# A two-block hybrid layer on one core: modulation tiles in four column groups, x queued behind two weight tiles, one statistics product

## The chip, the cores and the metric

One core of a Trainium2 chip. The metric is the device time of one execution in microseconds (us), the median of several runs. A profile comes from one execution, taken by the hardware profiler, and its span runs from the first to the last instruction. Engine names: PE is TensorE (matmuls), PEld its weight loads, DVE is VectorE, ACT is ScalarE, POOL is GpSimd, SP is SyncE, which here only issues DMAs. A letter q behind an engine means its queue.

## What is computed

Two transformer-like blocks over a sequence of 512 with width 1024, batch 1, all in f32. The change lies in the first steps of the first block, which are:

```python
cond = jax.nn.silu(c)
mod = cond @ w_ada[l] + b_ada[l]                      # 1024 -> 3072
shift, scale, gate = jnp.split(mod, 3, axis=-1)
h = rms_norm(x, norm_g[l]) * (1.0 + scale[:, None, :]) + shift[:, None, :]
proj = h @ w_in[l]
```

`proj` is split into the inputs of a state-space mixer (S5), of an attention with selected keys (an indexer scores the keys, the top 128 are kept), and of gates. The S5 mixer needs exp(lambda * dt) of complex parameters, and so a sine and a cosine of 1024 arguments. The rest of the first block and the second block (retention, gated linear attention, sliding-window attention, merging and a gated feed-forward) aren't touched by the change. `rms_norm` divides each position by the root of the mean of its squares over the width, plus an epsilon.

## The kernel before, in words

**Layout.** Activations are kept turned: the width lies on the 128 partitions in eight slabs (KT = 8) of 512 positions. All weights arrive as one stream of tiles of 1024 KB (128 partitions x 8 slabs x 256 columns), in the order of the list STAGES (line 64). The stream goes through three slots, `w_raw` (RAW_SLOTS = 3): SP issues the load of tile i when tile i - 3 has been used (L445 to L459). The first eight tiles are the shift and scale columns of `w_ada`, multiplied as they come ("raw"); of the others ACT makes a rounded high half (`split_high`, L1129) and DVE the rest (`split_low`, L1681), and a product is three matmuls: high by high, high by low, low by high. The first split tile is that of the key index (k_idx).

**Order of the work.** Each engine has its own program, written out by hand, and engines wait for each other by counting semaphores. Nothing reorders the work of an engine.

- **SP** (L435 to L464) issues ten small loads, then x (`xr`, 2048 KB, L443), then the stream (L445, L457).
- **POOL** (L468 to L511) sets constants, stores the small table of the relative bias (`bias_dram`), spreads it to 128 rows in DRAM (`bias_rows`, 2560 KB, L477), and then waits for the projected input of the state space (`u_act`).
- **PE** (L655 to L694): two products for the bias table into banks 4 and 5; then eight modulation tiles. `ada_rows` (L610) multiplies one tile: eight matmuls with one column of `silu_c` as weights and 256 moving columns; the result is one row on partition 0. Behind tile 0 stand the statistics products of slabs 0 to 3 of x (`stats_of`, L633: a 128x128 matrix of ones times the squares, which gives the sum over the width on all partitions), behind tile 1 those of slabs 4 to 7. Behind each odd tile from 3 on, `modulation` (L624) waits for ACT's copy of a finished pair of tiles (`mod_row`) and turns its 512 numbers from a row to columns, four matmuls with `turned` (L618). Then comes the product of k_idx (L672 to L687), each of whose eight steps waits for its slab of h (`act_low`), and the whole for the low half of its tile (`w_low`). The program's one matmul in f32 shows as two instructions in the trace.
- **ACT** (L1163 to L1192): the silu of c (L1164), two copies of the bias table, then eight squares of x into two buffers (`sqb`, L1143; the third waits until PE has used the first, and so on), then the two sines (L1174, L1175), for which DVE waits, then four row copies (`mrow`, L1185) with the root of the statistics behind the first, and the high halves of h (`input_high`, L1180) two by two, with the cast of the first split tile between the sixth and the seventh.
- **DVE** (L1721 to L1882): the S5 parameters up to the argument of the sines (L1721 to L1736), a wait for the sines (L1737), the rest of the setup up to `bb_im` (L1738 to L1765), the powers of lambda (L1767 to L1778), the reciprocal `rstd` (L1701), and a loop over four pairs of slabs (L1848): bias and gain (`modv`, `gs`), the values (`tval`, L1858) and, one slab behind, the low halves of h (`input_low`, L1844). The low half of the first split tile is made in its third round (L1862).

`PRESUM` (L329) lists the norms whose squares are added on DVE so that PE makes one product of the sum; norm0 isn't in it.

Of the kernel before, what the change touches and what calls it, by code (L numbers as in the profile page):

```python
# [19 lines left out]
P = 128  # L20
SEQ = 512
D = 1024
KT = D // P
TT = SEQ // P
WC = 256
# [131 lines left out]
def hybrid_blocks(nc, wstream, xT, vecs, consts, head_rows, onehot, rel_bias, ssm_vec, ssm_b, ssm_c, d_skip,  # L157
# [13 lines left out]
    with ctx:  # L171
# [48 lines left out]
        def placed(*tensors):  # L220
# [7 lines left out]
        (h_hi, h_lo, win_re, win_im, bb_re, bb_im, b_re, b_im, c_re, c_im, sv, pw_re, pw_im, tmp, btab, mrow, grow,  # L228
# [13 lines left out]
            (F0 + 74 * K, "mrow", [1, 2048], f32), (F0 + 48 * K, "grow", [1, 512], f32),  # L242
# [56 lines left out]
        c_ready, ada_done, mod_ready = sem("c_ready"), sem("ada_done"), sem("mod_ready")  # L299
# [29 lines left out]
        PRESUM = ("norm1", "post1", "norm2", "post2")  # L329
# [106 lines left out]
        def _(sp):  # L436
# [6 lines left out]
            sp.dma_start(xr[:, :, :], xT).then_inc(in_x, 16)  # L443

            for i, (kind, n, (_, _, kt, _)) in enumerate(STREAM):  # L445
                if kind == "split" and n == G["out1"][1].s:

                    sp.wait_ge(lg_ready, 32)
                    sp.dma_start(xr[:, :, :], xT).then_inc(x_reload, 16)
                if i >= RAW_SLOTS:  # L450
                    was, k, _ = STREAM[i - RAW_SLOTS]

                    if was == "split":
                        sp.wait_ge(*tile_used(k))
                    else:
                        sp.wait_ge(raw_used, k + 1)
                sp.dma_start(w_raw[:, i % RAW_SLOTS, 0:kt, :],  # L457
                             wstream[i][:, 0:kt * WC].rearrange("p (t c) -> p t c", c=WC)
                             ).then_inc(raw_loaded[i % RAW_SLOTS], 16)  # L459
# [8 lines left out]
        def _(pool):  # L468
            pool.memset(ones[:, :], 1.0).then_inc(consts_set, 1)
# [6 lines left out]
            pool.wait_ge(bias_stored, 16)  # L476
            pool.dma_start(bias_rows.ap(), bass.AP(bias_dram, 0, [[0, P], [1, HEADS * BIAS_LEN]])  # L477
# [37 lines left out]
        def _(pe):  # L515
# [101 lines left out]

            def turned(out, row):  # L618

                for m in range(4):  # L620
                    ins = mm(out[:, m:m + 1], row[0:1, m * P:m * P + P], ones[0:1, 0:1], True, True)
                ins.then_inc(ada_done, 1)
# [39 lines left out]
            for i in range(8):  # L662
                ada_rows("ada_shift_scale", i, bank[4 + i // 2][0:1, i % 2 * WC:i % 2 * WC + WC])
                if i == 0:
                    stats_of("norm0", ones[:, :], 0, 4)
                if i == 1:
                    stats_of("norm0", ones[:, :], 4, 8)
                if i % 2 and i > 1:
                    modulation(i // 2 - 1)
            modulation(3)  # L670
# [148 lines left out]
            for i in range(4):  # L819
                if i == 2:  # L820
                    pe.wait_ge(gate_row, 1)
                ada_rows("ada_gate", i, bank[3][0:1, i % 2 * WC:i % 2 * WC + WC])
                if i % 2:
                    pe.wait_ge(gate_row, i // 2 + 1)
                    pe.wait_ge(z_ready, 1)
                    turned(bank[4][:, 4 * (i // 2):4 * (i // 2) + 4], grow)
# [284 lines left out]
        def _(act):  # L1111
# [52 lines left out]
            act.activation(silu_c[:, :], vec[:, VEC["c"][0]:VEC["c"][1]], ACT.Silu).then_inc(c_ready, 1)  # L1164
# [4 lines left out]
            act.wait_ge(in_x, 16)  # L1169
            act.wait_ge(consts_set, 3)  # L1170
            for m in range(KT):
                square("norm0", m, xr[:, m, :])
            act.wait_ge(setup_trig, 1)
            act.activation(sv[:, 10, :], sv[:, 9, :], ACT.Sin).then_inc(trig_ready, 1)  # L1174
            act.activation(sv[:, 11, :], sv[:, 9, :], ACT.Sin, scale=0.5).then_inc(trig_ready, 1)  # L1175
            def input_high(m0, m1):
# [6 lines left out]
            for i in range(4):  # L1183
                act.wait_ge(raw_used, 2 * i + 2)
                act.copy(mrow[0:1, i * SEQ:(i + 1) * SEQ], bank[4 + i][0:1, :]).then_inc(mod_row, 1)  # L1185
                if i == 0:
                    root_of("norm0", D)
                if i >= 2:
                    input_high(2 * i - 4, 2 * i - 2)
            input_high(4, 6)  # L1190
            split_high(0)
            input_high(6, 8)  # L1192
# [434 lines left out]
        def _(dve):  # L1627
# [108 lines left out]
            dve.nop().then_inc(setup_trig, 1)  # L1736
            dve.wait_ge(trig_ready, 2)  # L1737
# [29 lines left out]
            settle(dve.memset(pw_re[:, 0, :], 1.0))  # L1767
            settle(dve.memset(pw_im[:, 0, :], 0.0))
            settle(dve.tensor_copy(pw_re[:, 1, :], lre))
            settle(dve.tensor_copy(pw_im[:, 1, :], lim))  # L1770
            n = 1
            while n < STEPS:
                top = (pw_re[:, n:n + 1, :].to_broadcast([P, n, PAIRS]),
                       pw_im[:, n:n + 1, :].to_broadcast([P, n, PAIRS]))
                cmul((pw_re[:, n + 1:2 * n + 1, :], pw_im[:, n + 1:2 * n + 1, :]),
                     (pw_re[:, 1:n + 1, :], pw_im[:, 1:n + 1, :]), top,
                     tmp[:, 0:n * PAIRS].rearrange("p (t j) -> p t j", j=PAIRS))
                n *= 2  # L1778
# [69 lines left out]
            for i in range(4):  # L1848
# [13 lines left out]
                if i == 2:  # L1862
                    split_low(0)
# [676 lines left out]
```

## Time and profile before

| | us |
|---|---|
| median of 3 runs (lowest, highest) | 1654.45 (1653.86, 1655.89) |
| the profiled execution | 1651.64 |
| its span, first to last instruction | 1649.5 |
| busy in the span: PE, PEld | 1574.7, 1232.4 |
| busy in the span: DVE, ACT, POOL | 888.2, 591.2, 23.1 |

The mean granted TensorE clock over the span is 0.978 of full speed. A busy PE isn't a PE at its peak, since matmuls are pipelined and their ends are modelled. In the timeline rows further down the columns are: start in us from the span's beginning, duration in us, engine, line, operation, output and inputs, shape, count (neighbours of one kind are merged), and in brackets how long the engine had been idle and what ended the wait.

### The profile page before, as it was taken

What the parts mean: (1) busy time and instruction counts of PE and PEld (TensorE: products, weight loads), DVE (VectorE), ACT (ScalarE), POOL (GpSimd) and SP (SyncE); (2) the same over time, 40 slices, a digit from 0 to 9 for tenths busy, and PEclk for the clock granted to TensorE, in tenths of its full rate; (3) what the DMA queues carried; (4) which work ended last, traced back from release to release, by engine and by line L of the source; (5) the groups of instructions that cost most, each with busy time, mean ns of one, the idle gap of its engine ahead of it and who ended that gap; (6) DMA issues with size and microseconds to landing.
All of it is one profiled execution on the core that took longest, in us unless ns stands there. A gap on an engine that the chain in (4) does not pass through costs nothing.

```text
span 1649.5 us, 19385 instructions
## 1 busy us (share of the span) xinstructions
PE 1574.7 (95%) x7876; PEld 1232.4 (75%) x7876; DVE 888.2 (54%) x1424; ACT 591.2 (36%) x867; POOL 23.1 (1%) x34
## 2 busy tenths in 40 slices
PE   6899999899999999999999999999998999999995
PEld 2476785666778788777788978888876888888884
DVE  3787899556572766343533535453346644444233
ACT  2333323354542656323434632333243322222220
POOL 0002010000000000000000000000000000000000
PEclk9899999999999999999999999999998999999998
DMA  8423144200442111121222222122231222222221
GB/s 300 147 78 103 52 81 139 92 26 4 177 152 97 57 65 65 52 77 61 71 106 103 77 77 66 63 93 87 102 141 64 103 98 82 101 103 96 96 90 51
DMA packets 23271, 152.24 MB, mean 92 GB/s; under 512 B 3328, under 2 KB 3888, under 8 KB 6912
## 3 DMA queue, kind: packets, MB, share of 16 engines
q1 hardware_dynamic: 20720, 137.43, 23.4%
q0 software_dynamic: 2464, 13.59, 2.9%
q8 instruction: 62, 1.02, 0.3%
q14 instruction: 25, 0.20, 0.0%
HBM read 144.55 MB, written 7.88 MB: 92 GB/s over the span
## 4 chain that ended last, share of the span: by engine, by line
PE 90%; DVE 7%; ACT 2%; issue 1%; DMA 1%; SPq 0%; DVEq 0%; ACTq 0%
PE bank L517 88%; DVE score L1898 1%; DVE small L1897 1%; PE bank L848 1%; PE bank L911 1%; DMA w_raw<-wstream 1%; DVE rstd L1701 0%; DVE sgb L1645 0%; DVE down L2455 0%; DVE w_lo L1681 0%; DVE score L1927 0%; DVE h_lo L1696 0%; DVE y_lo L1696 0%; DVE tval L2123 0%; ACT w_hi L1129 0%
## 5 line engine op out<-in xcount | busy, mean ns | idle before, releaser
L517 PE MATMUL bank<-h_hi,w_hi 128*128 128x512 f32 x1112 | 447.0, 402 | 19.1 <-DVE h_lo L2392 7.8
L517 PE MATMUL bank<-h_hi,w_lo 128*128 128x512 f32 x1128 | 443.4, 393 | 0.0
L517 PE MATMUL bank<-h_lo,w_hi 128*128 128x512 f32 x1112 | 437.0, 393 | 0.0
L1681 DVE TENSOR_TENSOR w_lo<-w_raw,w_hi 128x2048 fp32r<-128x2048 f32 (+2 forms) x109 | 245.4, 2253 | 252.3 <-ACT w_hi L1129 250.8
L1129 ACT CAST w_hi<-w_raw 128x2048 fp32r<-128x2048 f32 (+2 forms) x110 | 206.0, 1873 | 179.6 <-PE bank L517 176.8
L517 PEld LDWEIGHTS bank<-h_hi,w_hi 128*128 128x128 f32 x1112 | 211.2, 190 | 71.3 <-issue 18.9
L517 PEld LDWEIGHTS bank<-h_hi,w_lo 128*128 128x128 f32 x1128 | 213.5, 189 | 46.6
L517 PEld LDWEIGHTS bank<-h_lo,w_hi 128*128 128x128 f32 x1112 | 210.9, 190 | 44.5 <-issue 1.7
L517 PE MATMUL bank<-y_hi,w_hi 128*128 128x512 f32 x272 | 112.6, 414 | 3.7 <-DVE w_lo L1681 3.0
L517 PE MATMUL bank<-y_lo,w_hi 128*128 128x512 f32 x272 | 106.9, 393 | 0.0
L517 PE MATMUL bank<-y_hi,w_lo 128*128 128x512 f32 x272 | 106.8, 393 | 0.0
L517 PE MATMUL bank<-w_hi,h_hi 128*128 128x256 f32 x352 | 102.8, 292 | 0.0
L517 PE MATMUL bank<-w_hi,h_lo 128*128 128x256 f32 x352 | 100.9, 287 | 0.0
L517 PE MATMUL bank<-w_lo,h_hi 128*128 128x256 f32 x352 | 100.9, 287 | 0.0
L1408 ACT ACTIVATE sgb<-bank 128x512 f32<-128x512 f32 x40 | 23.9, 598 | 166.5 <-PE bank L517 166.5
L517 PEld LDWEIGHTS bank<-w_hi,h_hi 128*128 128x128 f32 x352 | 68.9, 196 | 7.3 <-issue 7.3
L517 PEld LDWEIGHTS bank<-w_lo,h_hi 128*128 128x128 f32 x352 | 69.0, 196 | 0.0
L517 PEld LDWEIGHTS bank<-w_hi,h_lo 128*128 128x128 f32 x352 | 68.9, 196 | 0.0
L517 PE MATMUL bank<-f_hi,w_hi 128*128 128x512 f32 x176 | 68.5, 389 | 0.0
L517 PE MATMUL bank<-f_lo,w_hi 128*128 128x512 f32 x176 | 68.5, 389 | 0.0
L517 PE MATMUL bank<-f_hi,w_lo 128*128 128x512 f32 x176 | 68.5, 389 | 0.0
L517 PEld LDWEIGHTS bank<-y_hi,w_hi 128*128 128x128 f32 x272 | 51.7, 190 | 17.6 <-issue 5.5
(351 smaller groups left out, 1915.6 us busy)
## 6 DMA issues: line engine op xcount, KB each, us to landing
w_raw<-wstream SPq DMA_DIRECT2D x120, 1024.0 KB, 4.8
xr<-xT SPq DMA_DIRECT2D x2, 2048.0 KB, 7.8
w_raw<-wstream SPq DMA_DIRECT2D x4, 768.0 KB, 4.2
bias_rows<-bias_table POOLq DMA_DIRECT2D x1, 2560.0 KB, 15.2
bias<-bias_rows POOLq DMA_DIRECT2D x1, 2048.0 KB, 8.9
x_saved<-xr POOLq DMA_DIRECT2D x1, 2048.0 KB, 9.3
xr<-x_saved POOLq DMA_DIRECT2D x1, 2048.0 KB, 8.0
outT<-down SPq DMA_DIRECT2D x8, 256.0 KB, 2.0
```

Of the source, the lines that this page charges most:

```text
L517: return pe.matmul(out, lhsT, rhs, start=start, stop=stop)
L848: ins = pe.transpose(bank[PT_BANKS[i % 2]][:, s * P:s * P + P], prob(i, qt)[:, s * P:s * P + P], ident)
L911: ins = pe.transpose(bank[ST_BANKS[t % 2]][:, j * P:j * P + P], lg[:, n % 2, j, kb * P:kb * P + P], ident)
L1129: act.copy(hi_of(s)[:, 0:kt, :], w_raw[:, i % RAW_SLOTS, 0:kt, :]).then_inc(w_high, 1)
L1408: act.activation(sgb[:, m % 2, :], bank[bk][:, :], func).then_inc(bank_free[bk], 1)
L1681: dve.tensor_tensor(w_low_of(s)[:, 0:kt, :], w_raw[:, i % RAW_SLOTS, 0:kt, :], hi_of(s)[:, 0:kt, :].bitcast(f32), ALU.subtract).then_inc(w ...
L1897: settle(dve.max(m8, s))
L1898: settle(dve.match_replace(s, m8, s, NEG_TAKEN))
```

## The change

It puts x behind two weight tiles in SP's order, and the broadcast of the bias rows behind the eighth modulation tile. The eight modulation tiles are multiplied in four column groups: the silu of c is laid out as `silu_w`, 32 columns per slab of which only the first isn't zero (POOL zeroes it, ACT copies the values in), and slab k goes to the 32 output partitions that start at 32 (k mod 4). `mrow` so has 128 rows, and the matmuls that turn it also sum over them. norm0 joins `PRESUM`: DVE adds the eight squares, PE makes one product. On ACT the sines stand ahead of the squares, and the row copies, the cast and the high halves have a new order. On DVE the additions stand ahead of the wait for the sines, the powers behind the first pair of slabs, and the first low half of weights behind the second pair.

```diff
-            (F0 + 74 * K, "mrow", [1, 2048], f32), (F0 + 48 * K, "grow", [1, 512], f32),
+            (F0 + 74 * K, "mrow", [P, 2048], f32), (F0 + 48 * K, "grow", [1, 512], f32),
+            (F0 + 66 * K, "silu_w", [P, KT, 32], f32),
...
-        PRESUM = ("norm1", "post1", "norm2", "post2")
+        PRESUM = ("norm0", "norm1", "post1", "norm2", "post2")
...
-            sp.dma_start(xr[:, :, :], xT).then_inc(in_x, 16)
 
             for i, (kind, n, (_, _, kt, _)) in enumerate(STREAM):
+                if i == 2:
+                    sp.dma_start(xr[:, :, :], xT).then_inc(in_x, 16)
...
         def _(pool):
+            pool.memset(silu_w[:, :, :], 0.0).then_inc(silu_zero, 1)
...
             pool.wait_ge(bias_stored, 16)
+            pool.wait_ge(raw_used, 8)
             pool.dma_start(bias_rows.ap(), bass.AP(bias_dram, 0, [[0, P], [1, HEADS * BIAS_LEN]])
...
+            def ada_groups(i, out):
+
+                tile, raw = G["ada_shift_scale"][i]
+                pe.wait_ge(raw_loaded[tile % RAW_SLOTS], 16 * (tile // RAW_SLOTS + 1))
+                for k in range(KT):
+                    rows = slice(k % 4 * 32, k % 4 * 32 + 32)
+                    ins = mm(out[rows, :], silu_w[:, k, :], w_raw[:, tile % RAW_SLOTS, k, :], k < 4, k >= 4)
+                ins.then_inc(raw_used, 1)
+
             def turned(out, row):
 
+                n = row.shape[0]
                 for m in range(4):
-                    ins = mm(out[:, m:m + 1], row[0:1, m * P:m * P + P], ones[0:1, 0:1], True, True)
+                    ins = mm(out[:, m:m + 1], row[:, m * P:m * P + P], ones[0:n, 0:1], True, True)
                 ins.then_inc(ada_done, 1)
...
             for i in range(8):
-                ada_rows("ada_shift_scale", i, bank[4 + i // 2][0:1, i % 2 * WC:i % 2 * WC + WC])
-                if i == 0:
-                    stats_of("norm0", ones[:, :], 0, 4)
-                if i == 1:
-                    stats_of("norm0", ones[:, :], 4, 8)
-                if i % 2 and i > 1:
+                ada_groups(i, bank[4 + i // 2][:, i % 2 * WC:i % 2 * WC + WC])
+                if i % 2 == 0 and i:
                     modulation(i // 2 - 1)
+                if i == 2:
+                    pe.wait_ge(presum_ready, 1)
+                    mm(stat_bank("norm0")[:, :], ones[:, :], rstd[:, :], True, True).then_inc(sq_used, 1)
             modulation(3)
...
-            act.activation(silu_c[:, :], vec[:, VEC["c"][0]:VEC["c"][1]], ACT.Silu).then_inc(c_ready, 1)
+            settle(act.activation(silu_c[:, :], vec[:, VEC["c"][0]:VEC["c"][1]], ACT.Silu))
+            act.wait_ge(silu_zero, 1)
+            act.copy(silu_w[:, :, 0:1], silu_c[:, :, None]).then_inc(c_ready, 1)
...
-            act.wait_ge(in_x, 16)
-            act.wait_ge(consts_set, 3)
-            for m in range(KT):
-                square("norm0", m, xr[:, m, :])
             act.wait_ge(setup_trig, 1)
             act.activation(sv[:, 10, :], sv[:, 9, :], ACT.Sin).then_inc(trig_ready, 1)
             act.activation(sv[:, 11, :], sv[:, 9, :], ACT.Sin, scale=0.5).then_inc(trig_ready, 1)
+            act.wait_ge(consts_set, 3)
...
-            for i in range(4):
+            def modulation_row(i):
+
                 act.wait_ge(raw_used, 2 * i + 2)
-                act.copy(mrow[0:1, i * SEQ:(i + 1) * SEQ], bank[4 + i][0:1, :]).then_inc(mod_row, 1)
-                if i == 0:
-                    root_of("norm0", D)
-                if i >= 2:
-                    input_high(2 * i - 4, 2 * i - 2)
-            input_high(4, 6)
+                act.copy(mrow[:, i * SEQ:(i + 1) * SEQ], bank[4 + i][:, :]).then_inc(mod_row, 1)
+
+            modulation_row(0)
+            act.wait_ge(in_x, 16)
+            for m in range(KT):
+                square("norm0", m, xr[:, m, :])
+            sqrt_table()
+            root_of("norm0", D)
+            modulation_row(1)
+            input_high(0, 2)
+            modulation_row(2)
+            input_high(2, 4)
             split_high(0)
-            input_high(6, 8)
+            modulation_row(3)
+            input_high(4, 8)
...
             dve.nop().then_inc(setup_trig, 1)
+            dve.wait_ge(sq_ready, 2)
+            dve.tensor_tensor(rstd[:, :], sqb[:, 0, :], sqb[:, 1, :], ALU.add).then_inc(sq_used, 2)
+            for m in range(2, KT):
+                dve.wait_ge(sq_ready, m + 1)
+                dve.wait_ge(sq_used, m)
+                dve.tensor_tensor(rstd[:, :], rstd[:, :], sqb[:, m % 2, :], ALU.add)\
+                   .then_inc(sq_used if m < KT - 1 else presum_ready, 1)
             dve.wait_ge(trig_ready, 2)
...
+            def powers():
+
+                settle(dve.memset(pw_re[:, 0, :], 1.0))
...
-                if i == 2:
+                if i == 0:
+                    powers()
+                if i == 1:
                     split_low(0)
```

The body of `powers` is the code of L1767 to L1778, unchanged. `sqrt_table` (L1152) is one activation of a single column with the square root.

## Rows read from the trace of the kernel before

**Rows 1.** The chain that ended last, 0 to 100 us: start us, us, what.

```profile
5.88 9.76 DMA w_raw<-wstream
...
15.77 39.25 PE bank L517 x160
```

**Rows 2.** Timeline: the load of x, and ACT's squares behind it.

```profile
5.40 0.43 SPq L443 DMA_DIRECT2D xr<-xT  x1
13.18 1.15 ACT L1143 ACTIVATE sqb<-xr 128x512 f32<-128x512 f32 x2 [4.74 <-DMA xr<-xT]
...
22.09 0.63 ACT L1143 ACTIVATE sqb<-xr 128x512 f32<-128x512 f32 x1 [7.76 <-PE bank L517]
```

**Rows 3.** Timeline: PE at tiles 0 and 1 and the last two turned rows.

```profile
15.77 5.22 PE L517 MATMUL bank<-w_raw,silu_c 128*1 128x256 f32 x16 [8.23 <-DMA w_raw<-wstream]
...
24.69 3.61 PE L517 MATMUL bank<-w_raw,silu_c 128*1 128x256 f32 x16
...
54.94 1.94 PE L517 MATMUL bank<-ones,mrow 1*128 1x1 f32 x16
```

**Rows 4.** Timeline: DVE from the argument of the sines to the first value.

```profile
16.25 0.17 DVE L1641 TENSOR_SCALAR sv<-sv 128x16 f32<-128x16 f32 x1
...
31.13 0.17 DVE L1638 TENSOR_TENSOR sv<-sv 128x16 f32<-128x16 f32 x1 [14.70 <-ACT sv L1175]
...
37.55 0.07 DVE L1767 MEMSET pw_re<- 128x16 f32 x1
...
42.38 3.35 DVE L1701 RECIPROCAL rstd<-root 128x512 f32<-128x512 f32 x1
...
45.77 0.16 DVE L1638 TENSOR_TENSOR modv<-bank,vec 128x4 f32<-128x4 f32 x1
...
46.17 1.42 DVE L1858 SCALAR_TENSOR_TENSOR tval<-xr,gs,rstd 128x512 f32<-128x512 f32 x2
```

**Rows 5.** Timeline: the start of the key-index product, and the last low halves of h.

```profile
64.46 0.79 PE L517 MATMUL bank<-h_hi,w_hi 128*128 128x512 f32 x1 [7.58 <-DVE w_lo L1681]
...
66.83 1.62 DVE L1844 SCALAR_TENSOR_TENSOR h_lo<-tval,modv,h_hi 128x512 fp32r<-128x512 f32 x2
```

**Rows 6.** The page's DMA issues: count, size of one, median us to landing.

```profile
w_raw<-wstream SPq DMA_DIRECT2D x120, 1024.0 KB, 4.8
...
bias_rows<-bias_table POOLq DMA_DIRECT2D x1, 2560.0 KB, 15.2
```

**Rows 7.** Timeline: ACT's first row copy, and the root behind it.

```profile
31.00 0.56 ACT L1185 COPY mrow<-bank 1x512 f32<-1x512 f32 x1
...
31.58 1.28 ACT L1149 ACT_TABLE_LOAD   x1
...
32.87 0.69 ACT L1149 ACTIVATE root<-bank,eps 128x512 f32<-128x512 f32 x1
```

**Rows 8.** Nearest operations: timeline of DVE and PE, then tile w_raw (min/median/max ns).

```profile
171.22 0.69 DVE L1638 TENSOR_TENSOR cos_t<-cos_t,sv 128x512 f32<-128x512 f32 x1
...
165.49 1.86 PE L517 MATMUL bank<-cst,sqb 128*128 128x2 f32 x8
...
L517 PE MATMUL bank<-w_raw,silu_c x128: 377/379/634, 15.8 to 54.6; 128*1 128x256 f32 x128
```

**Rows 9.** Timeline: values on DVE, a high half and the first cast on ACT.

```profile
57.34 0.75 DVE L1858 SCALAR_TENSOR_TENSOR tval<-xr,gs,rstd 128x512 f32<-128x512 f32 x1
...
58.79 0.75 DVE L1858 SCALAR_TENSOR_TENSOR tval<-xr,gs,rstd 128x512 f32<-128x512 f32 x1
...
59.57 0.72 ACT L1180 ACTIVATE h_hi<-tval,modv 128x512 fp32r<-128x512 f32 x1 [0.73 <-DVE tval L1858]
60.20 1.88 ACT L1129 CAST w_hi<-w_raw 128x2048 fp32r<-128x2048 f32 x1
```

**Rows 10.** Stretch 64 to 70 us: PE, PEld, DVE, ACT, POOL busy, PEclk, DMA share, GB/s.

```profile
64.00:70.00 6.00, 5.54 (x13) 4.38 (x14) 4.66 (x9) 3.23 (x3) 0.00 (x0) 0.50 0.00 0
```

**Rows 11.** Timeline of DVE: the low half of the fifth split tile.

```profile
108.51 2.29 DVE L1681 TENSOR_TENSOR w_lo<-w_raw,w_hi 128x2048 fp32r<-128x2048 f32 x1 [4.69 <-ACT w_hi L1129]
```

More of the change, by code:

```diff
@@ L227, in hybrid_blocks @@
         H0, X0, F0 = 0, 32 * K, 48 * K
-        (h_hi, h_lo, win_re, win_im, bb_re, bb_im, b_re, b_im, c_re, c_im, sv, pw_re, pw_im, tmp, btab, mrow, grow,
+        (h_hi, h_lo, win_re, win_im, bb_re, bb_im, b_re, b_im, c_re, c_im, sv, pw_re, pw_im, tmp, btab, mrow, grow, silu_w,
          down, xr, xa, xb, ga_, gb_, bias, merged,
@@ L298, in hybrid_blocks @@
         x_act, kr_psum, k_ready, heads_loaded = sem("x_act"), sem("kr_psum"), sem("k_ready"), sem("heads_loaded")
-        c_ready, ada_done, mod_ready = sem("c_ready"), sem("ada_done"), sem("mod_ready")
+        silu_zero, c_ready, ada_done, mod_ready = sem("silu_zero"), sem("c_ready"), sem("ada_done"), sem("mod_ready")
         setup_trig, trig_ready = sem("setup_trig"), sem("trig_ready")
@@ L825, in _ @@
                     pe.wait_ge(z_ready, 1)
-                    turned(bank[4][:, 4 * (i // 2):4 * (i // 2) + 4], grow)
+                    turned(bank[4][:, 4 * (i // 2):4 * (i // 2) + 4], grow[:, :])
             for gr in G["glu"]:
@@ L1765, in _ @@
                  (b_re[:, :, :], b_im[:, :, :]), tb)
[L1767 to L1778, printed above, removed]
+            def powers():
+                settle(dve.memset(pw_re[:, 0, :], 1.0))
+                settle(dve.memset(pw_im[:, 0, :], 0.0))
+                settle(dve.tensor_copy(pw_re[:, 1, :], lre))
+                settle(dve.tensor_copy(pw_im[:, 1, :], lim))
+                n = 1
+                while n < STEPS:
+                    top = (pw_re[:, n:n + 1, :].to_broadcast([P, n, PAIRS]),
+                           pw_im[:, n:n + 1, :].to_broadcast([P, n, PAIRS]))
+                    cmul((pw_re[:, n + 1:2 * n + 1, :], pw_im[:, n + 1:2 * n + 1, :]),
+                         (pw_re[:, 1:n + 1, :], pw_im[:, 1:n + 1, :]), top,
+                         tmp[:, 0:n * PAIRS].rearrange("p (t j) -> p t j", j=PAIRS))
+                    n *= 2
             def input_rows(half):
```

## The prediction

> **What bounds the kernel now.** I read the chain of waits first, because it says which engine's delays reach the end; then the timeline of the first 110 us, engine by engine, since every edit of the change lies there. The chain starts with a wait for the first weight tile until 15.6 us, then stays on the PE for 39 us, and after a gap goes on with the PE at 64.46 us [rows 1, 5]. In the timeline the reader is to see three things. First, the queue: x is issued ahead of the weight tiles and lands at 13.18 us, where ACT's wait for it ends [rows 2], so tile 0 lands only at 15.64. Second, the PE: a modulation tile is 16 instructions and takes 3.6 us [rows 3], eight of them with eight statistics products between; ACT's squares, two buffers deep, wait for those products, and the two sines stand behind the squares, so DVE sits idle 14.7 us for them [rows 4]. Third, DVE: from the sines on it has the setup of the state space, the powers and the reciprocal to do one after another, 31.13 to 45.77 us [rows 4]. What follows is paced by the modulation products. So the PE bounds the stage today, with DVE not far behind it. The event to be dated is the start of the key-index product at 64.46 us, where the PE has waited 7.58 us for the low half of the first split weight tile [rows 5].
>
> **The change part by part, as a timetable of the new kernel.**
>
> *Queue.* SP issues tiles 0 and 1, then x, then tile 2. The bytes up to the end of x and of the two tiles are the same in either order. x (2048 KB) landed 2.46 us before tile 0 (1024 KB), so a tile costs 2.46 us of the queue [rows 1, 2]. Tile 0 then lands at 13.18 - 2.46 = 10.7, tile 1 at 13.2, x at 13.18 + 2 x 2.46 = 18.1, tile 2 at 20.6. x is thus 4.9 us later. The 2560 KB broadcast of the bias table [rows 6] leaves this stretch and comes behind the eighth tile.
>
> *Modulation tiles.* Same 16 instructions per tile, now in four column groups. No row shows such matmuls side by side. Bounds: all four at once, a quarter of 3.6, 0.9 us, or 1.8 at half the clock; one after another, 3.6 or 7.2. I take 1.8, nearest to an engine that starts from idle each time, as the first tile did (5.22 against 3.61, [rows 3]). Tiles 0 and 1 are done by 15.0. What hides these tiles is told below.
>
> *Sines.* DVE's setup up to the argument ends at 16.42 [rows 4]; ACT is free from 8.4, 4.74 before x lands today [rows 2], and does both sines by 16.9, the first row copy (0.56 today, [rows 7]) by 17.5, and is ready for x at 18.1. The copy now reads 128 partitions for one; the rows nearest, ACT operations of 128x512, are at 0.6 to 0.7 (the root, 0.69 [rows 7]). The silu copy and the memset are a few tenths before 10.7, covered by the wait for tile 0.
>
> *Squares and pre-sum.* A pair of squares takes 1.15, one alone 0.63 [rows 2]; an addition of 128x512 on DVE 0.69, with its semaphore 0.73 [rows 8]. With two buffers: the first addition runs from 19.3 to 20.0; the third square can start only then, and ends at 20.65; six additions at 0.72 follow it, since from there ACT keeps up. The seventh ends at 25.0. It adds 7 additions to DVE and takes 7 of 8 products off the PE. The one product that stays runs with a wait in front of it: behind it on the PE are tiles 3 to 7, so they start at about 26.8. The root (table load 1.28 and 0.69, [rows 7]) is ready by 27.6.
>
> *DVE, the new path.* Since the additions stand ahead of the setup, all of this begins at 25.0: the setup without the powers, 31.13 to 37.5, 6.4 us, to 31.4 (the root has long been there); the reciprocal with its wait 3.39, to 34.7 [rows 4]; the first pair: modulation and gain 0.40 [rows 4], value, high half, low half, 0.75 + 0.72 + 0.04, and 0.68 until the next may issue, to 37.3 [rows 9]; the powers, now behind the first pair, 42.38 - 37.55 = 4.8 [rows 4], to 42.2; the second pair, 0.40 and 1.45 to its second value, whose end is 0.78 later, to 44.8 [rows 9]. Then ACT's high half starts; the cast of the split tile starts 0.63 behind it, and the PE 4.26 behind that [rows 5, 9]: 44.8 + 4.9 = **49.7**. That is 14.8 earlier than 64.46.
>
> *Is the PE ready?* Row copy 2 (counted from 0) now stands behind the first two high halves: values to 36.6, high half to 37.3, copy to 37.9. The PE waits there before tile 7, which ends at about 41.5; its load, issued when tile 4 is used, at about 30, takes some 5 [rows 6] and is there. Row copy 3 stands behind the cast, 47.3 to 47.9; its turned products take 1.0 us (16 instructions in 1.94, [rows 3]), or 1.86 after idling, as eight small products with 128x128 weights do in [rows 8]: done at 49.0 to 49.8, just in time. The tiles are off the path: this part costs nothing while a tile stays under some 3.4 us. If that cover goes, the loss is worked out under the rivals.
>
> *The key-index product.* Today its first 13 matmuls fill 5.54 us, 0.43 apart, at a granted clock of 0.50, the lower level, 1.2 GHz [rows 10], after the PE had been idle since 56.9 [rows 3]. The new one starts from the same idleness, so I give it the same 13. But its later operands come at the pace of DVE: the low halves 3 to 7 are ready from 51.4 to 56.9, where today the last is at 68.45 [rows 5]. At 1.28 per step the PE reaches step 4 at 54.8 and step 7 at about 57; the eighth low half comes at the same time. At most 0.2 us is lost: lead **14.6**.
>
> *Behind it.* DVE's own lead at its last low half is only 68.45 - 56.9 = 11.6, since the pairs after the first split now run back to back. It isn't passed on: DVE's next nearest wait is for the cast at 108.51, where it idles 4.69 us today because the PE is late [rows 11]. 3.0 of that is used up. The weight tiles before it stay in time: the key-index product ends at 49.7 + 13 x 0.43 + 35 x 0.226 = 63.2, and the next low half (cast at 56.0, behind the last high half) is there at 60.2; the one behind it, after 7.5 us of input rows, at 70, against 74. After that all engines are 14.6 earlier, the selection of keys included. The broadcast of the bias rows, issued at about 41.5, lies beside one weight tile that isn't cast before 63 us, and its result is not read before the middle of the first block: nothing. POOL's queue behind it waits for the PE's input product anyway.
>
> **Sum.** 1651.64 - 14.6 = 1637.0 for an execution like the profiled one; that one is 2.81 below the median of the three, so against 1654.45 it is 1639.8.
>
> **The rule of the skill on this.** The trace has each small matmul at 379 ns in the median but starts 0.22 apart [rows 3, 8]: today they overlap in the pipe of one group. The Trainium skill, "TensorE: Matmul & The Clock Gate", Part 3, says that matmuls placed in different column groups run at the same time, at 2.38 times for three. "TensorEngine Tiling (Array Packing)", Key Properties, speaks against the change: going from one tiling mode to another drains the engine. By the first the sum stands; by the second, if it were paid at each instruction, rival B would hold. No row here shows either.
>
> **The rivals.**
> A. *The groups run one after another, at the high clock.* A tile then is 3.5 us; tile 0 takes 5.2, to 15.9, tile 1 ends at 19.4, the row copy at 20.0, and the squares start 1.9 late. All else shifts with them; the PE's last tile, at 47, still hides. 1641.7. For: no row shows side by side. Against: nothing holds them in order but the pipe.
> B. *The groups hold the PE up, and it ends slower: each instruction waits for the one before to leave the array.* At the high clock, 16 x 0.379 = 6.1 us a tile [rows 8]. From 10.7: three tiles to 29, then a product of turned rows and the statistics, five tiles, three turned sets and a copy: about 65.3, within 1 us of today. It turns the sign from 6.0 us a tile on. With an array that so keeps falling idle at the lower clock, 0.43 between starts or more, 6.9 us a tile, the same sum gives 75: 10.6 us slower, 1665.
> C. *Part of the lead is lost behind the start*: the key-index product stays at the lower clock for all 24 matmuls (11 x 0.2 = 2.3), or DVE's lead of 11.6 is what counts because a wait behind 69 us isn't covered. 1642 to 1643. For: [rows 10] shows how much clock a short idleness costs, and later stages have such stretches too, whose place may shift by a us or two either way.
> D. *x is late.* Each us that x lands behind 18.1 is a us lost, one for one.
>
> **How the numbers follow.** The forecast 0.62, A 0.12, C and D 0.18, B 0.04 equal and 0.04 slower. A measurement of this kernel tells 0.2%, 3.3 us, from no change; all but B are beyond it: faster 0.92, same 0.04, slower 0.04. The range takes in A and C with a D of 2 us above, 1646, and below a clock that comes back early in the key-index product and later (2 us) with x half a us early and 2 us of spread between sets of runs: 1635.
>
> **What would show it.** Right: x landing near 18.1; squares from 18.1; DVE never idle from 25 to 45 but for short handovers; the reciprocal near 31.4; the PE's wait for mrow before tile 7; the key-index product at 49.7 with the wait for w_lo or mrow in front of it. Starts of a tile's matmuls under 0.1 us apart show the groups at once, 0.2 show A, 0.38 B. Wrong: a statistics product or a tile as the last thing before the key-index product, squares that wait for the row copy, or a difference at the start that is not found again at 290 us, behind the selection of keys.

## The result, and the profile after

The changed kernel takes 1639.16 us in the median of 4 runs (1637.93 to 1641.64), the kernel before 1654.15 (1653.82 to 1655.89) beside it. The ratio is 0.9907, with a 95% interval of 0.9892 to 0.9922: faster by 0.9%, 15.0 us. Timed again later with five rounds it gave 1639.71 against 1653.27, ratio 0.9918 (0.9906 to 0.9931). The forecast was 1639.8, faster.

The page of the changed kernel, its totals:

```profile
span 1639.9 us, 19378 instructions
...
PE 1559.6 (95%) x7862; PEld 1228.3 (75%) x7862; DVE 893.4 (54%) x1431; ACT 591.7 (36%) x869; POOL 23.3 (1%) x35
```

The profiled execution took 1641.64 us, the slowest of its four, while that of before, 1651.64, lies below all four that the changed kernel was timed beside. The two traces are therefore 10.0 us apart where the medians are 15.0 apart. So I compare dates of events, not totals. First the chain of waits of the changed kernel (start us, us, what):

```profile
6.35 13.68 DMA xr<-xT
20.05 1.16 ACT sqb L1156 x2
21.31 0.70 DVE rstd L1758
```

The chain that began with tile 0 [rows 1] now begins with x. The timeline of the changed kernel's PE:

```profile
12.82 1.94 PE L521 MATMUL bank<-w_raw,silu_w 128*32 128x256 f32 x16 [5.39 <-DMA w_raw<-wstream]
15.17 1.64 PE L521 MATMUL bank<-w_raw,silu_w 128*32 128x256 f32 x16 [0.42 <-DMA w_raw<-wstream]
22.57 1.93 PE L521 MATMUL bank<-w_raw,silu_w 128*32 128x256 f32 x16 [5.76 <-DMA w_raw<-wstream]
...
27.42 2.08 PE L521 MATMUL bank<-rstd,ones 128*128 128x512 f32 x2 [1.12 <-DVE rstd L1762]
...
34.18 1.07 PE L521 MATMUL bank<-w_raw,silu_w 128*32 128x256 f32 x16
...
50.21 1.87 PE L521 MATMUL bank<-ones,mrow 128*128 128x1 f32 x8 [6.32 <-ACT mrow L1198]
52.05 0.80 PE L521 MATMUL bank<-h_hi,w_hi 128*128 128x512 f32 x1
```

A tile of 16 instructions took 3.61 us and takes 1.07 at the high clock (the tile at 34.18, granted clock 1.00) or 1.93 at the low one (the tile at 22.57, granted clock 0.50, after 5.76 us of waiting). The first tile, at 12.82, is as long, 1.94, though the clock recorded for it is 1.00; so I go by durations there. At 1.07 us for 16, instructions of 0.38 us start less than 0.1 apart: the four groups do work at once. Between its pieces of work the PE now waits for others: for tiles, for DVE and, 6.32 us, for the last row copy. The timelines of ACT and DVE, in order of time:

```profile
16.94 0.58 ACT L1198 COPY mrow<-bank 128x512 f32<-128x512 f32 x1 [0.23 <-PE bank L521]
20.05 1.15 ACT L1156 ACTIVATE sqb<-xr 128x512 f32<-128x512 f32 x2 [2.52 <-DMA xr<-xT]
...
29.60 0.69 ACT L1162 ACTIVATE root<-bank,eps 128x512 f32<-128x512 f32 x1 [1.64 <-PE bank L521]
...
22.70 4.67 DVE L1762 TENSOR_TENSOR rstd<-rstd,sqb 128x512 f32<-128x512 f32 x6 [0.70 <-ACT sqb L1156]
...
33.68 3.35 DVE L1721 RECIPROCAL rstd<-root 128x512 f32<-128x512 f32 x1
...
49.71 2.29 DVE L1701 TENSOR_TENSOR w_lo<-w_raw,w_hi 128x2048 fp32r<-128x2048 f32 x1 [1.91 <-ACT w_hi L1142]
```

DVE has no wait over 0.2 us from 22.70 until the second pair of low halves is issued: it is the bound, as forecast, and x is what starts it. At the end two things come together: behind the cast of the split tile (47.80) its low half on DVE ends at 52.00, and the row copy and its turned products end on the PE at 52.05. The reciprocal starts 8.7 us earlier than in [rows 4], the key-index product 12.4 earlier than in [rows 5].

### The profile page after: what moved, and what is told of

It reads as the page before. It is cut to its first block, busy times and chain, and to the rows that moved or that the text cites. A ratio compares the mean times of both kernels' runs of the same rounds, so it can differ in the third digit from the quotient of the medians.

```text
span 1639.9 us, 19378 instructions
## 1 busy us (share of the span) xinstructions
PE 1559.6 (95%) x7862; PEld 1228.3 (75%) x7862; DVE 893.4 (54%) x1431; ACT 591.7 (36%) x869; POOL 23.3 (1%) x35
## 4 chain that ended last, share of the span: by engine, by line
PE 91%; DVE 5%; ACT 2%; issue 1%; DMA 1%; SPq 0%; DVEq 0%; ACTq 0%
PE bank L521 89%; DMA xr<-xT 1%; PE bank L924 1%; PE bank L861 1%; DVE rstd L1721 1%; DVE sgb L1665 0%; DVE down L2486 0%; DVE score L1958 0%; DVE h_lo L1716 0%; DVE rstd L1762 0%; DVE tval L2154 0%; ACT w_hi L1142 0%; ACT sgb L1256 0%; ACT sqb L1156 0%; DVE sqb L2045 0%
## 5 line engine op out<-in xcount | busy, mean ns | idle before, releaser
L521 PE MATMUL bank<-h_hi,w_hi 128*128 128x512 f32 x1112 | 448.5, 403 | 11.5 <-DVE h_lo L2423 7.8
## 6 DMA issues: line engine op xcount, KB each, us to landing
x_saved<-xr POOLq DMA_DIRECT2D x1, 2048.0 KB, 10.1
```

What stands on the lines that cost most here:

```text
L521: return pe.matmul(out, lhsT, rhs, start=start, stop=stop)
```

## The experiments

Twelve runs. The table gives, from each profiled execution: when ACT starts the squares (but for one group, where it is told below, the landing of x), DVE the reciprocal, and PE the key-index product; then the time of that execution, the median, and the ratio to the kernel before with its interval. All times in us. (Changed = the changed kernel.)

| kernel | squares | recipr. | key index | profiled | median | ratio |
|---|---|---|---|---|---|---|
| before | 13.18 | 42.38 | 64.46 | 1651.64 | 1654.15 | |
| changed | 20.05 | 33.68 | 52.05 | 1641.64 | 1639.16 | 0.9907 (0.9892, 0.9922) |
| one group | 20.82 | 34.43 | 52.81 | 1640.90 | 1642.33 | 0.9933 (0.9914, 0.9952) |
| groups alone | 14.70 | 39.22 | 55.88 | 1643.90 | 1643.61 | 0.9943 (0.9924, 0.9961) |
| x alone | 19.97 | 33.59 | 51.97 | 1637.00 | 1637.98 | 0.9906 (0.9883, 0.9928) |
| powers later | 19.61 | 33.22 | 46.72 | 1636.36 | 1634.64 | 0.9886 (0.9862, 0.9910) |
| x first | 13.84 | 28.79 | 47.16 | 1635.36 | 1637.28 | 0.9904 (0.9888, 0.9921) |
| x first, powers later | 13.89 | 29.68 | 43.72 | 1628.47 | 1630.45 | 0.9863 (0.9843, 0.9883) |
| bias early | 18.52 | 33.95 | 52.33 | 1637.38 | 1638.36 | 0.9914 (0.9891, 0.9937) |
| eight products | 19.43 | 35.92 | 54.31 | 1641.09 | 1643.56 | 0.9937 (0.9922, 0.9952) |
| x first, one group | 14.26 | 31.66 | 51.99 | 1639.34 | 1639.55 | 0.9916 (0.9903, 0.9930) |
| changed again | 18.58 | 32.20 | 50.57 | 1638.34 | 1639.71 | 0.9918 (0.9906, 0.9931) |
| x first again | 14.91 | 29.15 | 47.53 | 1638.61 | 1638.41 | 0.9909 (0.9896, 0.9923) |
| x first, powers later again | 14.32 | 28.70 | 43.18 | 1627.82 | 1632.85 | 0.9877 (0.9861, 0.9892) |

Read across the rows: in the changed kernel, x alone and changed again the key-index product starts 32.00, 32.00 and 31.99 us behind the first square. In this kernel what is behind x is one chain of constant length; I use it below to price the edits that leave x behind two tiles, whatever x did in that run. With x first the additions wait for DVE's own setup, and the chain is counted from the first addition.

**One group.** All matmuls of a tile go to the first 32 rows of the bank.

```diff
-                    rows = slice(k % 4 * 32, k % 4 * 32 + 32)
-                    ins = mm(out[rows, :], silu_w[:, k, :], w_raw[:, tile % RAW_SLOTS, k, :], k < 4, k >= 4)
+                    rows = slice(0, 32)
+                    ins = mm(out[rows, :], silu_w[:, k, :], w_raw[:, tile % RAW_SLOTS, k, :], k == 0, k == KT - 1)
```

> The changed kernel with all eight matmuls of a modulation tile in one column group (32 columns each, output partitions 0 to 31), nothing else new. In the changed kernel a tile is 1.1 to 1.9 us, tile 0 is used at 14.8, tile 1 at 16.8, the first row copy ends at 17.5, x lands at 20.05 and the key-index product starts at 52.05. Theory (DVE's path from the squares on bounds, the tiles are hidden but for the first two): tile 0 takes 5.2 as in the kernel before, tile 1 3.6, row copy at 22.2, squares 2.1 later, key-index product at 54.2, all later tiles hidden. Rival (the groups carry the gain): each tile is paid, 8 x 2.5 us or more, key-index product at 62 or later.

Its PE timeline, then ACT's:

```profile
11.84 8.40 PE L521 MATMUL bank<-w_raw,silu_w 128*32 128x256 f32 x32 [4.40 <-DMA w_raw<-wstream]
...
46.88 3.64 PE L521 MATMUL bank<-w_raw,silu_w 128*32 128x256 f32 x16
...
20.33 0.57 ACT L1198 COPY mrow<-bank 32x512 f32<-32x512 f32 x1 [2.69 <-PE bank L521]
20.82 1.14 ACT L1156 ACTIVATE sqb<-xr 128x512 f32<-128x512 f32 x2
```

and its load of x (issue in us, then the us to landing):

```profile
L447 SPq DMA_DIRECT2D xr<-xT x1: 432/432/432, 6.3 to 6.3; - x1
...
DMA to landing us min/median/max: 12.7/12.7/12.7
```

A tile costs 3.64 us, 3.4 times the 1.07 of four groups. x landed at 6.3 + 12.7, about 19.0, but the squares have no wait for it in front of them: they start at 20.82, behind the row copy, which waited 2.69 us for tiles 0 and 1. So one group costs 1.8 us of start here. The rest of the tiles is covered: behind the first square the chain is 31.99 us, as with four groups. The median is 2.6 to 3.2 us above the changed kernel's two, 1.8 of it explained; the rest isn't.

**Groups alone.** The kernel before with only the four groups: x first, eight statistics products, squares before sines, the old order on DVE.

```diff
-                ada_rows("ada_shift_scale", i, bank[4 + i // 2][0:1, i % 2 * WC:i % 2 * WC + WC])
+                ada_groups(i, bank[4 + i // 2][:, i % 2 * WC:i % 2 * WC + WC])
```

> The kernel before with the column groups alone: x first, eight statistics products, sines behind the squares, old orders on ACT and DVE, bias rows early. Theory (PE bounded the stage before; without its tiles DVE's path behind the sines does): sines at about 25.5 instead of 30.8, first values at 40, the split tile's cast behind the sixth high half at 48.6, key-index product at about 53, so nearly the whole gain (11.5 us of 12.4). Rival (the reordering carries the gain): the product starts no earlier than 60, because the squares, the sines or the loads beside the bias rows hold it.

Its PE timeline:

```profile
19.16 4.98 PE L519 MATMUL bank<-sqb,ones 128*128 128x512 f32 x8
24.07 1.07 PE L519 MATMUL bank<-w_raw,silu_w 128*32 128x256 f32 x16
25.07 3.83 PE L519 MATMUL bank<-sqb,ones 128*128 128x512 f32 x8
...
55.88 0.80 PE L519 MATMUL bank<-h_hi,w_hi 128*128 128x512 f32 x1 [8.10 <-DVE w_lo L1695]
```

Here the groups pay 8.6 us of start by the dates of the two traces, since in the old order the tiles stand on the path, before the products that release the squares. That understates them: x landed 1.5 us later than in the kernel before (14.70 against 13.18), and tile 0 as well (17.29 against 15.77). Behind the first square the product starts after 41.18 us instead of 51.28, which is 10.1. I had expected 11.5. So the same edit is worth 8.6 to 10.1 us here and 1.8 in the changed kernel, by what stands around it.

**x alone in the queue.** SP waits for x before it issues tile 2.

```diff
                 if i == 2:
                     sp.dma_start(xr[:, :, :], xT).then_inc(in_x, 16)
+                    sp.wait_ge(in_x, 16)
```

> The changed kernel in which SP waits for x to land before it issues tile 2. In the changed kernel x lands at 20.05, forecast was 18.1. Theory (a load that is queued behind shares the DMA engines with the one before it and delays its end): x lands at about 18.1, squares and all of DVE's path 1.9 earlier, key-index product at 50.1; tile 2 lands at about 23, before the PE needs it. Rival (the rate of the small loads and tiles themselves was overrated): x lands at 20.0 as before, tile 2 at 24.9, no gain.

x landed at 19.97, no earlier: the rival was right, and in this run x's lateness is not a matter of sharing with tile 2. Tile 2 came at 24.87, 4.9 behind x where in the changed kernel it is 2.5 behind; it was covered.

**Powers later.** The table of powers goes behind the low half of the second split tile, the third split tile's ahead of the input rows.

```diff
-                if i == 0:
-                    powers()
...
-            input_rows(0)
-            split_low(2)
+            powers()
...
+            split_low(2)
+            input_rows(0)
```

> The changed kernel with the powers of lambda moved from behind the first pair of slabs to behind the second split tile's low half, and the third low half ahead of the input rows. Theory (DVE's path bounds the start, and its 3 to 5 us of room behind it take the powers): key-index product at 52.05 - 4.8 = 47.2, and a lead of 4.8 that is still there at 115 us. Rival 1 (another engine is next): the product starts no earlier than 50, with the PE waiting for the turned rows. Rival 2 (no room behind): the start is 4.8 earlier but the PE waits for w_lo, wi or win_re before 100 us and gives it back.

The wait in front of the product's turned rows fell from 6.32 to 1.45 us in its PE timeline, and the gain at the start passed on:

```profile
44.88 1.86 PE L521 MATMUL bank<-ones,mrow 128*128 128x1 f32 x8 [1.45 <-ACT mrow L1198]
46.72 0.79 PE L521 MATMUL bank<-h_hi,w_hi 128*128 128x512 f32 x1
```

The chain behind x is 27.11 us, 4.9 shorter, which is the powers' length (39.71 to 44.54 in the changed kernel). It shows that DVE's own work sets the start there.

**x first.** The changed kernel with x ahead of the weight tiles again, two squares before the sines, the row copy behind the squares.

```diff
+            sp.dma_start(xr[:, :, :], xT).then_inc(in_x, 16)
...
-                if i == 2:
-                    sp.dma_start(xr[:, :, :], xT).then_inc(in_x, 16)
...
-            modulation_row(0)
...
+            modulation_row(0)
```

> The changed kernel with one part undone: x is issued ahead of the weight tiles again, the first two squares stand ahead of the sines, and the first row copy stands behind all squares. Theory (the start is bounded by x, squares and additions, so putting x behind two tiles costs time): x lands at 13.2 to 14.7 us instead of 20.05, DVE's setup up to the sines ends near 16.4 and the seven additions of 0.79 end near 22.5 instead of 27.37; the key-index product starts near 47.3 instead of 52.05, and the time is 4 to 5 us under the changed kernel. Rival (the first tiles bound the start, as the place of x in the changed kernel supposes): tile 0 lands at 15.6 to 17.3, its modulation rows and the first row copy are late, and the key-index product starts at 52 or later. Third possibility: the chain of the tiles, low clock and 1.9 us each, takes over in part, and the start is between 48 and 51.

Its timelines of ACT, DVE and PE:

```profile
13.84 1.15 ACT L1155 ACTIVATE sqb<-xr 128x512 f32<-128x512 f32 x2 [5.70 <-DMA xr<-xT]
...
16.38 0.69 DVE L1759 TENSOR_TENSOR rstd<-sqb 128x512 f32<-128x512 f32 x1 [0.22 <-DVE sv L1662]
17.82 4.67 DVE L1763 TENSOR_TENSOR rstd<-rstd,sqb 128x512 f32<-128x512 f32 x6 [0.76 <-ACT sqb L1155]
...
16.25 1.94 PE L520 MATMUL bank<-w_raw,silu_w 128*32 128x256 f32 x16 [9.01 <-DMA w_raw<-wstream]
...
47.16 0.79 PE L520 MATMUL bank<-h_hi,w_hi 128*128 128x512 f32 x1
```

The first addition waits for DVE's own setup, no longer for x, and the start is 4.9 us before the profiled changed kernel's, as the theory said to 0.2. With groups and the pre-sum in place, putting x behind two tiles costs at the start; it does not pay. The edit also moves two squares and a row copy on ACT, so it prices that order together with x's place. In the median it brought 1.9 us and not the 4 to 5 expected, though the two profiled executions are 6.3 apart.

**x first and powers later.** The two edits together, no other.

> The kernel of x first with one more edit: the powers stand behind the second split weight tile, the third in front of the input rows, as in the run of the later powers. Theory (the two gains add, since both shorten DVE's own chain): reciprocal and first pair 4.8 us earlier and the second pair 4.8 us earlier still, the key-index product near 42.5 us, about 9.5 us before the changed kernel's, 1630 us. Rival (another chain takes over): the modulation tiles 5 to 7, each 1.9 us at the low clock with a landing every 2.5 to 3 us, or the row copies between ACT's high halves, end last; the start is then at 45 to 47, no better than with the later powers alone, and the wait in front of the key-index product names the row copy instead of the low half.

43.72 instead of 42.5. About 0.9 of the difference lies before the chain: DVE's small loads landed later in this execution, and its first addition starts at 17.25 instead of 16.38. For the rest ACT's timeline shows the next bound, the landing of the first split weight tile:

```profile
39.44 1.90 ACT L1141 CAST w_hi<-w_raw 128x2048 fp32r<-128x2048 f32 x1 [0.43 <-DMA w_raw<-wstream]
```

In the repeat the first addition starts at 16.29, that wait is 0.87, and the product starts at 43.18. It is the fastest version here.

**Bias early.** POOL doesn't wait for the eighth tile before the broadcast of the bias rows.

```diff
-            pool.wait_ge(raw_used, 8)
```

> The changed kernel without POOL's wait for the eighth tile: the 2560 KB broadcast of the bias table is issued near 14 us again. Theory (the transfers share one rate, so what is issued beside x delays it): x lands 3 to 6 us later, at 23 to 26 instead of 20.05, and the key-index product starts 3 to 6 us later, 55 to 58; the time is 3 to 6 us above the changed kernel. Rival (the broadcast is held back by its own queue or fits beside x, as the 13.2 us of x in the kernel before allow): x lands within 1 us of 20.05 and nothing changes.

Its timelines of POOL, ACT and PE:

```profile
8.58 0.65 POOL L478 DMA_DIRECT2D bias_table<-btab  x1 [7.32 <-ACT btab L1181]
...
18.52 1.15 ACT L1155 ACTIVATE sqb<-xr 128x512 f32<-128x512 f32 x2 [0.25 <-DMA xr<-xT]
...
33.16 0.69 ACT L1161 ACTIVATE root<-bank,eps 128x512 f32<-128x512 f32 x1 [6.74 <-PE bank L520]
...
27.42 1.93 PE L520 MATMUL bank<-w_raw,silu_w 128*32 128x256 f32 x16 [11.86 <-DMA w_raw<-wstream]
```

The theory fell in its place and half held in its price. x was not late at all, but the run does not test whether a transfer beside x would delay it: the queue of the broadcast, issued at 14.78, moved 0.08 MB before x landed at 18.52, and 2.44 of the 3.24 MB that all queues moved from then to 27.4. Tile 2 was late: it landed 8.9 us behind x instead of 2.5, 6.4 more, and 2560 KB at 2.46 us for 1024 would be 6.2. The statistics product stands behind tile 2 on the PE, so the root came at 33.16, behind the setup, and the chain behind x grew from 32.0 to 33.8. The total moved by less than its spread.

**Eight products.** The pre-sum undone: no additions on DVE, eight statistics products behind tile 2.

```diff
-                    pe.wait_ge(presum_ready, 1)
-                    mm(stat_bank("norm0")[:, :], ones[:, :], rstd[:, :], True, True).then_inc(sq_used, 1)
+                    stats_of("norm0", ones[:, :], 0, 8)
```

> The changed kernel with the pre-sum undone: no additions on DVE, eight statistics products on the PE behind tile 2, one for each square. Theory (DVE's chain sets the start; the PE's products at the low clock cost less than the additions): DVE's setup is done before the statistics and no longer stands behind them; squares come 0.65 us apart from 20.05, and the eighth product, 1.7 us each at the low clock or 0.9 at the high one, ends at 29 to 36; root and reciprocal follow without the setup's 6.4 us, and the key-index product starts between 47 and 53, most likely 1 to 3 us before the changed kernel's 52.05. Rival (the pre-sum is worth its additions): eight products at the low clock hold tiles 3 to 7 back as well, these end last, and the start is at 54 or later, 2 to 5 us slower.

Its timelines of PE, ACT and DVE:

```profile
25.52 9.24 PE L521 MATMUL bank<-sqb,ones 128*128 128x512 f32 x16
...
27.61 0.63 ACT L1155 ACTIVATE sqb<-xr 128x512 f32<-128x512 f32 x1 [7.04 <-PE bank L521]
...
35.92 3.35 DVE L1720 RECIPROCAL rstd<-root 128x512 f32<-128x512 f32 x1 [12.87 <-ACT root L1161]
```

The rival was right in its date, not in its ground: the chain behind x is 34.9, 2.9 longer, and both medians of the changed kernel are some 4 us lower, but the tiles behind the products don't end last. The 2.9 are there by the reciprocal, 16.5 us behind the first square instead of 13.6. I had not seen that the third square waits 7.04 us for a product that stands behind tile 2 and its turned rows. What the pre-sum buys is not fewer products; it unties the squares from the PE's queue.

**x first, one group.** The first experiment's edit on top of x first.

> The kernel of x first with all modulation matmuls in one column group, as in the run of one group: a tile costs 3.64 us. Theory (the groups pay where tiles stand on the path): x lands near 13.8 and the additions end near 22.5 as with x first, but tiles 0 to 2, from 16.3, end at 27.2, and the statistics product behind them reads the squares at 28 to 29; root at 30, reciprocal at 30.5 instead of 28.79, tiles 3 to 7 back to back until 47: the key-index product starts at 49.5 to 51, 2 to 4 us later than with x first and four groups, where with x behind two tiles one group cost 0.8. Rival (the tiles stay covered): within 1 us of 47.16.

Its PE timeline:

```profile
16.67 12.07 PE L520 MATMUL bank<-w_raw,silu_w 128*32 128x256 f32 x48 [9.01 <-DMA w_raw<-wstream]
...
30.70 7.09 PE L520 MATMUL bank<-w_raw,silu_w 128*32 128x256 f32 x32
37.73 1.05 PE L520 MATMUL bank<-ones,mrow 32*128 32x1 f32 x8
38.70 7.09 PE L520 MATMUL bank<-w_raw,silu_w 128*32 128x256 f32 x32
...
51.99 0.50 PE L520 MATMUL bank<-h_hi,w_hi 128*128 128x512 f32 x1
```

From 16.67 to 50.35, the end of the last tile, the PE is never idle for more than a few tenths: it is the bound, and the start is 4.8 us later than with four groups (4.5 against the repeat), a little more than the 2 to 4 expected, against 1.8 with x behind two tiles. The total is only 1.1 to 2.3 us above the two medians of x first.

**Changed, x first and the fastest version again**, beside each other on one chip, with five rounds.

> The changed kernel itself, timed beside the others of this call on one chip. Expected: x lands between 19 and 20.1, the key-index product starts between 51 and 52.1, the time is between 1637 and 1640, 1.5 to 3 us above x first and 7 to 10 above x first with the powers later. Rival: the profiled 1641.64 of the first set is the usual case, and the median is above 1640.

> The kernel of x first once more, beside the changed kernel on one chip. Theory (x ahead is earlier by 4.9 us at the start, whole to the end but for clock stretches of 1 to 2 us): 2 to 5 us below the changed kernel of the same call. Rival (its start is given back behind it): within 1 us of it.

> x first and the powers later once more. Theory: the key-index product near 43.7 us, held by the landing of the first split weight tile near 39.4; the time 7 to 10 us below the changed kernel of the same call, 1629 to 1632. Rival: the 1630.45 was a chance of few runs, and it is above 1633.

Several expectations were missed by a little: x landed at 18.58 where 19 to 20.1 was expected, the changed kernel's product started at 50.57 where 51 to 52.1 was, and x first was 1.3 us below the changed kernel where 1.5 to 3, or 2 to 5, was. The fastest version came at 1632.85, where 1629 to 1632 was expected.

x first was 1.3 us below the changed kernel here and 1.9 below in the first sets, within the spread, though its trace starts the product 3.0 us earlier. The lead is there until 270 us: the PE's second set of turned gate rows starts at 273.11 in the changed kernel and 270.19 with x first. At 306 us it is gone: the first three turned attention weights start at 305.59 and 305.83. The stretches between, first of the changed kernel (columns: stretch, its length, busy time of PE, PEld, DVE, ACT, POOL, PEclk, DMA share, GB/s):

```profile
270.00:280.00 10.00, 7.02 (x30) 4.56 (x28) 7.23 (x11) 3.75 (x4) 0.00 (x0) 0.83 0.45 157
280.00:290.00 10.00, 8.97 (x40) 7.08 (x38) 4.50 (x5) 4.62 (x6) 0.00 (x0) 1.00 0.36 111
290.00:300.00 10.00, 9.02 (x31) 6.47 (x32) 2.86 (x12) 4.11 (x6) 0.00 (x0) 0.83 0.25 99
```

and of x first:

```profile
270.00:280.00 10.00, 7.30 (x24) 5.90 (x25) 4.77 (x6) 4.00 (x5) 0.00 (x0) 0.66 0.29 106
280.00:290.00 10.00, 7.99 (x36) 6.36 (x35) 5.14 (x6) 5.27 (x5) 0.00 (x0) 0.99 0.43 137
290.00:300.00 10.00, 10.00 (x30) 7.03 (x28) 2.23 (x10) 2.88 (x6) 0.00 (x0) 0.67 0.17 73
```

At 0.50 for the low level, granted clocks of 0.66 and 0.67 are 13 us at half speed, 0.83 twice are 7: some 3 us of work lost, which is as much as went. That the clock is the cause is argued from this sum; no run changes the clock alone. Nor is the loss a property of x first: in the first pair of traces its lead of 4.9 had grown to 8.0 at the same gate rows (277.52 and 269.53) and was 6.8 at the same attention weights (308.93 and 302.13). The fastest version kept its gain: 6.9 us below the changed kernel beside it, 7.4 at the start.

## Why the prediction was right

**The total** was 1639.8 and came out at 1639.16 and 1639.71. Step by step it was less exact than that.

*Queue.* The price of a tile held: tile 2 came 2.5 us behind x, x 7.2 us behind tile 0 (forecast 7.4). The step that missed is the anchor: x's landing in one execution, 13.18, was taken as fixed. In the seven traces with x first it landed from 13.18 to 14.91, mean 14.2; in the seven with x behind two tiles from 18.5 to 20.05, mean 19.3. The forecast 18.1 lies below all of the latter. The difference of the means, 5.1, bears out the forecast's 4.9. That was rival D, one for one, worth 1.95 us in the profiled run and 0.5 in the repeat.

*Tiles.* 1.8 us taken, 1.93 at the low clock. Rivals A and B fell: 16 instructions in 1.07 us start less than 0.1 us apart, and the same 16 in one group take 3.64. Rival A's price was right all the same: made to run one after another, the tiles let the squares start 1.8 us late, where 1.9 was worked out, and all else of them stayed covered.

*The two tiling rules.* The Trainium skill, "TensorE: Matmul & The Clock Gate", Part 3, says that small matmuls in different column groups run at the same time; this case agrees, with 3.64 us against 1.07, 3.4 times for four groups. The Trainium skill, "TensorEngine Tiling (Array Packing)", Key Properties, says that a change of tiling mode drains the engine; no row shows a cost of it: in the changed kernel the tile of 22.57 us is modelled to end at 24.50, and the turned rows start at 24.44.

*Additions.* 0.72 each was forecast, 0.79 measured (4.67 for six, last of them 0.70). The row used was of additions that wait for nothing; here each hands its buffer to a square and gets one back. This is 0.4 of the 2.35 us by which the start was late; x is the other 1.95.

*DVE's path.* 24.7 us were forecast from the end of the additions to the key-index product, 49.7 - 25.0; from 27.37 to 52.05 it is 24.7. The root was ready at 30.29, 2.7 us later than the forecast 27.6, and 2.4 of that is the late end of the additions; its product took 2.08 us at a granted clock of 0.50, but the table load ran beside it and not behind it. 3.4 us of setup still covered the root, and in the run with the bias early no longer did.

*Low clock at the product.* The product starts at the low clock as before, and its evacuation begins 8.25 us behind its start (8.50 before). As forecast, it costs nothing more.

*Behind it.* The forecast named a difference that is not found again at 290 us as a sign of being wrong. It is found: behind the selection of keys, the first product of queries and keys starts at 306.15 in the kernel before, at 294.28 in the changed kernel and at 290.98 in its repeat, 11.9 and 15.2 us earlier, where the starts were 12.4 and 13.9 earlier. Rival C so took 0.5 in one trace and gave in the other. A lead of 12.4 at the start is 12.5 at 98.96 us, where ACT's first write of the block's next result stood at 111.49. DVE's last low half of h led by 9.2 only, and the waits behind it took up the difference: the 4.69 of [rows 11] is 3.26, the ones at 80.49 and 91.92 in the kernel before, 1.21 and 0.88, are gone. This is the changed kernel's row:

```profile
95.97 2.29 DVE L1701 TENSOR_TENSOR w_lo<-w_raw,w_hi 128x2048 fp32r<-128x2048 f32 x1 [3.26 <-ACT w_hi L1142]
```

*The sum.* A start 14.8 earlier was forecast and 12.4 to 13.9 came. That the median still met the number is partly luck: from the start of 12.4 alone it would be 1641.8, 2.6 above the measured 1639.16; for the repeat, 13.9 gives 1639.4 against 1639.71. "Time less start of the key-index product" is 1587.2 in the profiled kernel before and runs from 1584.6 to 1591.1 in the 13 traces of the other kernels, mean 1587.4, through stretches of low clock. The forecast counted on 1587.2 for a profiled run and added 2.8 for the median; here the trace was the slowest of its four instead.

*The parts.* The forecast saw the change as one timetable and was right to: groups alone bring 8.6 us of start (10.1 behind x), where the whole brings 12.4; taken back out of the whole they cost 1.8, or 4.8 with x first. The pre-sum is worth 2.9 in the whole. The order of x, which I had only costed, is the one part that takes away: 3.0 to 4.9 at the start, together with ACT's order that goes with it, and 1.3 to 1.9 in the median, which is within the spread. The later broadcast spares 1.8 behind x, too little to see in the total. The sines' new place alone was not tried.

## What to carry to other kernels

Date the first event that all engines wait for, and ask of each part what it waits for in the new order: the same edit, the column groups, was worth 8.6 to 10.1, 4.8 or 1.8 us. A chain behind one landing can be known to 0.01 us from trace to trace while the landing itself wanders by 2, so forecast the landing from several executions. When a stage is shortened, look at once for the next bound: here x, then DVE's powers, then a weight tile, and taking the first two steps gave a kernel of 1630.45 and 1632.85 us, 1.2 to 1.4% under the kernel before.

## What was not expected

- The broadcast of 2560 KB, issued at 14.78 us while x was still under way, did not delay x (18.52) but the tile behind it, by 6.4 us: its queue moved next to nothing in its first 3.7 us. In the kernel before it was issued at 14.13, when x had landed (13.18). So no run here shows it beside x.
- Four column groups gave 3.4 times, not 4: a quarter of 3.64 would be 0.91, and a tile takes 1.07.
- In one pair of traces a start 3.0 us earlier was gone at 306 us, with as much more time at the low clock; in another pair a start 4.9 earlier had grown to 8.0 by 270 us. The edit doesn't touch the work there.
